# Attention values with their high and low parts side by side in one 128-column weight, and a new step order

## The reference

```
def one_block(qblk):                       # for each block of 128 queries
    sc = einsum('bqhgd,bkhd->bhgqk', qblk, k) * scale
    p = softmax(sc, axis=-1)
    return einsum('bhgqk,bkhd->bqhgd', p, v)

ya = blocked_attention(qa, ka, va, 1 / sqrt(64))
yb = blocked_attention(qb, kb, vb, 1 / sqrt(96))
merged = g_a * (ya @ w_branch_a) + g_b * (yb @ w_branch_b)
```

## Time and profile before

| what | value |
|---|---|
| median of 3 runs | 2993.85 us (2993.54 to 2993.94) |
| the profiled execution | 2993.22 us, its span 2991.4 us |
| PE busy | 2829.0 us, 95% of the span |
| DVE busy | 1614.9 us, 54% |
| ACT busy | 1147.8 us, 38% |
| POOL busy | 748.1 us, 25% |
| the chain that ended last | PE 86%, DVE 8%, ACT 2% |
| mean granted TensorE clock | 0.972 of full |

### The profile page before, as it was taken

One profiled execution on the slowest core, in us unless ns is written; L12 is line 12 of the kernel. 1 busy time (PEld: TensorE's weight loads), 2 busy tenths in 40 slices (PEclk: granted clock), 3 DMA queues, 4 the chain that ended last, 5 costly groups with the idle time before them and its releaser, 6 DMA issues.

```text
span 2991.4 us, 33731 instructions
## 1 busy us (share of the span) xinstructions
PE 2829.0 (95%) x12862; PEld 2317.4 (77%) x12862; DVE 1614.9 (54%) x2065; ACT 1147.8 (38%) x1758; POOL 748.1 (25%) x607
## 2 busy tenths in 40 slices
PE   8899999999998999999999967999999999999997
PEld 6677887888776778788887766878887789878886
DVE  5786446334367854453434895455533558555533
ACT  5675334222346753332223343322322348422221
POOL 2563113213025621140223161022200014122200
PEclk9999999999999999999999888999999989999999
DMA  3011322233220112223332201222232210123332
GB/s 136 28 43 43 99 92 85 94 97 99 85 85 22 43 53 95 85 92 99 99 95 87 79 19 60 92 92 95 96 106 99 83 52 1 57 92 99 99 103 88
DMA packets 75634, 236.68 MB, mean 79 GB/s; under 512 B 9776, under 2 KB 18240, under 8 KB 75488
## 3 DMA queue, kind: packets, MB, share of 16 engines
q1 hardware_dynamic: 74288, 231.31, 23.9%
q0 software_dynamic: 928, 3.27, 0.3%
q10 hardware_dynamic: 272, 0.06, 0.0%
HBM read 228.31 MB, written 2.10 MB: 77 GB/s over the span
## 4 chain that ended last, share of the span: by engine, by line
PE 86%; DVE 8%; ACT 2%; issue 1%; POOL 1%; DMA 1%; SPq 1%; DVEq 0%; POOLq 0%; ACTq 0%
PE bank L1800 27%; PE bank L1802 27%; PE bank L1801 27%; PE bank L2097 2%; PE bank L1961 1%; DVE S5S L1668 1%; DMA RAWW<-weights 1%; DVE STAT L1494 1%; PE bank L2003 1%; DVE S5S L1659 1%; SPq L817 1%; DVE WL L1383 1%; ACT WH L1072 1%; PE bank L1903 0%; DVE PHL L1388 0%
## 5 line engine op out<-in xcount | busy, mean ns | idle before, releaser
L1383 DVE TENSOR_TENSOR WL<-RAWW,WH 128x1024 fp32r<-128x1024 f32 (+2 forms) x424 | 573.7, 1357 | 862.5 <-ACT WH L1072 862.4
L1800 PE MATMUL bank<-UH,WH 128*128 128x512 f32 (+1 forms) x1920 | 762.3, 397 | 53.7 <-DVE UL L1393 29.4
L1801 PE MATMUL bank<-UL,WH 128*128 128x512 f32 (+1 forms) x1920 | 754.5, 393 | 0.0
L1802 PE MATMUL bank<-UH,WL 128*128 128x512 f32 (+1 forms) x1920 | 754.0, 393 | 0.0
L1072 ACT ACTIVATE WH<-RAWW 128x1024 fp32r<-128x1024 f32 (+2 forms) x424 | 433.9, 1027 | 368.5 <-DMA RAWW<-weights 368.0
L1800 PEld LDWEIGHTS bank<-UH,WH 128*128 128x128 f32 (+1 forms) x1920 | 364.6, 190 | 141.6 <-issue 58.1
L1801 PEld LDWEIGHTS bank<-UL,WH 128*128 128x128 f32 (+1 forms) x1920 | 365.0, 190 | 78.2 <-issue 2.4
L1802 PEld LDWEIGHTS bank<-UH,WL 128*128 128x128 f32 (+1 forms) x1920 | 364.4, 190 | 77.6
L1800 PE MATMUL bank<-HH,WH 128*128 128x512 f32 x512 | 199.2, 389 | 0.0
L1801 PE MATMUL bank<-HL,WH 128*128 128x512 f32 x512 | 199.2, 389 | 0.0
L1802 PE MATMUL bank<-HH,WL 128*128 128x512 f32 x512 | 199.2, 389 | 0.0
(11 more groups left out here) (340 smaller groups left out, 4711.2 us busy)
## 6 DMA issues: line engine op xcount, KB each, us to landing
RAWW<-weights SPq DMA_DIRECT2D x424, 512.0 KB, 3.4
X<-x SPq DMA_DIRECT2D x8, 256.0 KB, 5.4
FF<-tables POOLq DMA_DIRECT2D x2, 1024.0 KB, 7.2
U<-S5U SPq DMA_DIRECT2D x16, 128.0 KB, 2.4
GEL<-U SPq DMA_DIRECT2D x128, 16.0 KB, 1.8
out<-FF SPq DMA_DIRECT2D x8, 256.0 KB, 2.0
S5B<-s_b POOLq DMA_DIRECT2D x1, 512.0 KB, 4.3
S5C<-s_c POOLq DMA_DIRECT2D x1, 512.0 KB, 4.3
```

Source lines behind the costliest of these rows:

```text
L1383: dve.tensor_tensor(slot_words(WL, c % SLOTS, size), slot_words(RAWW, c % SLOTS, size), f32(slot_words(WH, c % SLOTS, size)), ALU.subtract ...
L1800: nc.tensor.matmul(out_, w[0], x_[0], start=start, stop=False, **how)
L1801: nc.tensor.matmul(out_, w[0], x_[1], start=False, stop=False, **how)
L1802: return nc.tensor.matmul(out_, w[1], x_[0], start=False, stop=stop, **how)
```

## The change

Of one head, the 64 columns of high value parts and the 64 columns of low parts now stand side by side in one weight of 128 columns (VS, MVS). Two products per key tile (`pair`: this weight with the high and with the low part of the probabilities) take the place of three, and OUTB then holds the result of the high values in 64 rows and that of the low values in the other 64. The two halves are added: ACT copies the low half across into a tile (`att_out_side`), DVE adds the other half from the bank (`att_out_sum`). After every second head ACT makes the high part of all 128 rows (`att_out_hi`) and POOL the low part (`att_out_lo`), where before ACT and DVE did this for each head. POOL's zeroing of MVH and MVL is gone. In the order, `att_lo` moves from behind the values to the start of a step, the exponential becomes a step of its own (`att_exp`) behind the transposes, and the transposes stand ahead of `att_normalise`. The gate phase's first products with QH, QL and with YBH, YBL get a wait for the low parts of their own.

```diff
# attention_steps: the order of the steps
-    for x in range(n + 8):
+    for x in range(n + 10):
         h, phase = divmod(x - KT - 4, KT)
         if 0 <= h < 2 * HEADS and phase == 3:
-            plan.add("att_out_hi", h=h, pv=h)
+            plan.add("att_out_side", h=h, pv=h)
+        if 2 <= h <= 2 * HEADS and h % 2 == 0 and phase == 1:
+            plan.add("att_out_lo", h=h - 1, p=whole.p)
...
+        if 4 <= x <= n + 3:
+            plan.add("att_lo", u=x - 4, h=(x - 4) // KT, t=(x - 4) % KT)
         if x < n:
             plan.add("att_scores", "u", h=x // KT, t=x % KT)
+        if 3 <= x <= n + 2:
+            plan.add("att_transpose", u=x - 3, h=(x - 3) // KT, t=(x - 3) % KT)
+        if x < n:
+            plan.add("att_exp", u=x)
         if 1 <= x <= n:
             plan.add("att_normalise", u=x - 1)
-        if 3 <= x <= n + 2:
-            plan.add("att_transpose", u=x - 3, h=(x - 3) // KT, t=(x - 3) % KT)
...
-        if 4 <= x <= n + 3:
-            plan.add("att_lo", u=x - 4, h=(x - 4) // KT, t=(x - 4) % KT)
         if 0 <= h < 2 * HEADS and phase == 3:
-            plan.add("att_out_lo", h=h, pv=h)
+            plan.add("att_out_sum", h=h, pv=h)
+        if 2 <= h <= 2 * HEADS and h % 2 == 0 and phase == 0:
+            whole = plan.add("att_out_hi", "p", h=h - 1, pv=h - 1)
# tiles
-        VH = at("VH", A0 + 20, [P, KT, P], F32R)
-        VL = at("VL", A0 + 22, [P, KT, P], F32R)
+        VS = at("VS", A0 + 20, [P, KT, 4, HD], F32R)
+        FIRST_SUM = at("FIRST_SUM", A0 + 32, [P, SEQ])
...
-        MVH = at("MVH", A0 + 60, [P, 2, KT, P], F32R)
-        MVL = at("MVL", A0 + 64, [P, 2, KT, P], F32R)
+        MVS = at("MVS", A0 + 60, [P, 2, KT, 2, HD], F32R)
...
+        def out_sum(st):
+
+            return SPARE[:, 0, :] if st.h >= 2 else FIRST_SUM[:]
# POOL
-                elif st.kind == "mla_mm" and st.h == 0:
-                    value_zeros(l)
...
+                elif st.kind == "att_out_lo":
+                    h, lo_, _, k = pv_place(st.h)
+                    pool.wait_ge(y_h.sem, y_h.after(l, st.p))
+                    pool.tensor_tensor(lo_[:, k, :], out_sum(st), f32(h[:, k, :]), ALU.subtract).then_inc(y_l.sem, 1)
# ACT
-                elif kind == "att_scores":
+                elif kind == "att_exp":
...
+                elif kind == "att_out_side":
+                    rows = pv_place(st.h)[2]
+                    other = slice(HD - rows.start, P - rows.start)
+                    act.wait_ge(pv.sem, pv.after(l, st.pv))
+                    if st.h >= 2:
+                        act.wait_ge(y_l.sem, y_l.after(l, st.h // 2 - 1))
+                    act.activation(out_sum(st)[rows, :], OUTB[other, :], ACT.Copy).then_inc(y_side.sem, 1)
                 elif kind == "att_out_hi":
                     h, _, rows, k = pv_place(st.h)
-                    act.wait_ge(pv.sem, pv.after(l, st.pv))
-                    act.activation(h[rows, k, :], OUTB[rows, :], ACT.Copy).then_inc(y_h.sem, 1)
+                    act.wait_ge(y_sum.sem, y_sum.after(l, st.pv))
+                    act.activation(h[:, k, :], out_sum(st), ACT.Copy).then_inc(y_h.sem, 1)
# DVE
-                elif kind == "att_out_lo":
-                    h, lo_, rows, k = pv_place(st.h)
-                    dve.wait_ge(y_h.sem, y_h.after(l, st.pv))
-                    rest(lo_[rows, k, :], OUTB[rows, :], h[rows, k, :]).then_inc(y_l.sem, 1)
+                elif kind == "att_out_sum":
+                    rows = pv_place(st.h)[2]
+                    dve.wait_ge(y_side.sem, y_side.after(l, st.pv))
+                    dve.tensor_tensor(out_sum(st)[rows, :], OUTB[rows, :], out_sum(st)[rows, :], ALU.add).then_inc(y_sum.sem, 1)
# PE
+            def pair(out_, w, x_, start, stop, **how):
+
+                nc.tensor.matmul(out_, w, x_[0], start=start, stop=False, **how)
+                return nc.tensor.matmul(out_, w, x_[1], start=False, stop=stop, **how)
...
-                            pe.wait_ge(y_l.sem, y_l.after(l, st.h - 1))
-                    if st.h == HEADS and st.keys[0] == 0:
-                        pe.wait_ge(mv_zero, l + 1)
+                            pe.wait_ge(y_sum.sem, y_sum.after(l, st.h - 1))
...
-                        v = (VH[:, k, :], VL[:, k, :]) if st.h < HEADS else (MVH[:, st.h % 2, k, :], MVL[:, st.h % 2, k, :])
-                        ins = product(OUTB[:], v, (ph[:, k, :], pl[:, k, :]), k == 0, k == KT - 1)
+                        i = st.h % 2
+                        v = VS[:, k, 2 * i:2 * i + 2, :] if st.h < HEADS else MVS[:, i, k, :, :]
+                        ins = pair(OUTB[:], v.rearrange("p a n -> p (a n)"), (ph[:, k, :], pl[:, k, :]), k == 0, k == KT - 1)
```

More of the change, by code:

```diff
@@ L683, in build @@
         mats_cut = ctx.enter_context(nc.semaphore("mats_cut"))
-        mv_zero, k_zero = (ctx.enter_context(nc.semaphore(k)) for k in ("mv_zero", "k_zero"))
+        k_zero = ctx.enter_context(nc.semaphore("k_zero"))
         x_done = signal("x_done", "x", DT)
@@ L706, in build @@
         probs_h, probs_l = signal("probs_h", "u"), signal("probs_l", "u", 2)
-        pv, y_h, y_l = signal("pv", "pv"), signal("y_h", "pv"), signal("y_l", "pv")
+        pv, y_side, y_sum = (signal(k, "pv") for k in ("pv", "y_side", "y_sum"))
+        y_h, y_l = signal("y_h", "p"), signal("y_l", "p")
         gate = signal("gate", "ge")
@@ L833, in layer_inputs @@
                 ins.then_inc(k_zero, 1)
-            def value_zeros(l):
-                pool.wait_ge(pv.sem, pv.after(l, U_HEADS - 1))
-                for k in range(2):
-                    for v in (MVH, MVL):
-                        ins = pool.memset(f32(v[:, k, :, HD - k * HD:P - k * HD]), 0.0)
-                ins.then_inc(mv_zero, 1)
             def add_squared(l, k, again):
@@ L1832, in linear_job @@
                     for k in range(kt):
-                        if st.first:
+                        if st.first or st.half == 0 and i == k == 0:
                             pe.wait_ge(*ready(k0 + k))
```

31 lines of the change are left out of this document (15 added, 16 removed).

## The result

The changed kernel takes 3013.39 us, median of 4 runs (3013.26 to 3014.44), against 2993.69 for the kernel before in the same runs: a ratio of 1.0065, 95% interval 1.0053 to 1.0078. It is slower by 20 us where 7 to 8 were forecast, and lies 0.4 us above the range.

What follows compares the result with a forecast made beforehand. In the seven MLA loops a DVE-ACT-POOL loop without PE work was taken to bind, nearly level with PE. Per layer -2.5 + 8.0 - 1.5 = +4.0 us, +8 for both: 2993.2 + 8 = 3001 us, range 2982 to 3013.

Steps and rivals of the forecast that it cites:

- Until the first MQL: Each layer's stretch before the first MQL: fewer products, POOL's new instruction and the order together -2.5 us, bounds -5.7 and 0.
- The prediction's own sign: Before the first MQL: this part is wrong if PE's wait at the long L1444 (3.93 us) shrinks instead of growing.
- The seven loops: First MQL to last, per layer: order +2.9 and POOL's low part +5.0, together +8.0 us, bounds +4.0 and +11.
- Its signs: In the trace after, MQL starts about 12.9 and 14.1 us apart in turn, against 12.36.
- The order's term: In the loops: a second PHL before the second reciprocal, 6 x 0.7 less 1.3 of vanished waiting, +2.9 us.
- POOL's term: In the loops: `att_out_lo` inside POOL's unbroken work in four of seven, 4 x 1.26, +5.0 us.
- the sum above has that at x = 17 alone: POOL holding up RL, WL and L1444, DVE's two-SBUF-input steps, was counted only at x = 17, before the loops.
- No removed product lies in them: The seven loops: none of the removed products was taken to lie there, so nothing gained once PE is ahead.
- After the last MQL: Last MQL to gates, per layer: products -2.8 us, new wait for the sum and high part +1.3, together -1.5.
- is hidden: At the gates: POOL's last low part, 1.26 us, covered by 48 products, 11 us, before QH is read.
- the term of -2.8 us for the removed products: After the last MQL: 12 of the 64 removed products, PE bound or nearly so, save 2.8 us.
- a rival about the loops: Clock rival: PE idles at each MQL, half-clock spells lengthen loops, 14 us more, 3013 to 3015 us; chance 0.08.

Runs made afterwards that it cites:

- two_products: Kernel before without the product of low values and high probabilities; 2985.23 us, ratio 0.9970.
- order_only: Kernel before with only the new order of the steps of a key tile; 3006.27 us, ratio 1.0037.
- low_on_dve: Changed kernel with the low part of a pair's sum made on DVE instead of POOL, at the same step; 3007.07 us, ratio 1.0043.
- low_later: Changed kernel with POOL's low part moved behind the first normalisation, last pair unmoved, two sum tiles in turn; 2999.32 us, ratio 1.0013.
- rl_psum: Changed kernel with RL of the MLA heads made from PSUM tile TURN instead of SBUF tile FF; 3003.48 us, ratio 1.0031.
- low_twice: Changed kernel with POOL making the low part twice for the MLA pairs, once into an unused tile; 3023.34 us, ratio 1.0090.
- fill_after: Changed kernel with the product of values and low probabilities issued twice, giving PE its former work; 3019.03 us, ratio 1.0078.
- old_order: Changed kernel with the steps of a key tile in their former order; 3008.73 us, ratio 1.0046.
- values_only: Changed kernel with the former order of steps and the low part on DVE; 3016.73 us, ratio 1.0068.

## Why the prediction was wrong in size

**Until the first MQL: the number came, the working didn't.** -2.5 forecast and measured in layer 0, -2.0 in layer 1. The kernels that change one part at a time put it together otherwise: two_products alone gives -1.4 for the 3.4 us counted for products, order_only gives -1.9 for 0.3, and moving the low part from POOL to DVE (low_on_dve, first MQL at 161.28) gives back none of the 1.26 charged for it. The prediction's own sign speaks against the step too: PE's wait of 3.93 us behind the long L1444 is gone. The same instruction, L1455 now, takes 0.80 us for 3.59, and PE has several shorter waits instead (1.35 at 123.94, 1.21 at 127.90, 2.11 at 131.81). That the sum came out is luck.

```profile
120.94 0.80 DVE L1455 SCALAR_TENSOR_TENSOR CF<-CF,LP,RCQ 128x512 f32<-128x512 f32 x1
```

**The seven loops: right in cause, mis-sized**, +8.0 for +10.2. Its signs came: MQL 13.2 to 13.5 us apart without a low part and 13.9 to 14.5 with one, for 12.9 and 14.1. The two terms share POOL's row and can't be told apart in one way only. By the place of the low part (changed kernel against low_later) it costs 6.4 us for 5.0, and the rest of the change 3.9 (90.4 for 86.5) for 2.9. By the order alone (order_only) the order costs 5.9, and what comes on top 4.3. Both ways miss the same thing. The order's term had one effect of the order, the second PHL, which the trace shows (0.7 us) and which costs some 0.25 us a loop at most, as far as the runs tell. It left out RL, which now meets POOL's unbroken row: in all seven loops of order_only, and in the three loops of the changed kernel without a low part, at 2.1 to 2.8 us. rl_psum takes 0.9 us off each of these three. In the four others ACT makes the pair's whole high part ahead of RH, RL comes later and takes 1.1 us. POOL's term had the low part's length, and the dose of low_twice confirms that (1.24 and 1.23). It left out that the row then runs into WL, 0.5 us in three loops. The prediction had the rule for both, with RL and WL named, and put it at nothing beside L1444: "the sum above has that at x = 17 alone". That is the step that failed. The Trainium skill, SBUF — State Buffer, Who interferes with whom, says a DVE instruction with two SBUF inputs contends with a GpSimd instruction that reads SBUF; 2.79 us with FF and 0.68 with TURN at the same place agree. The section gives no price for a DVE instruction that meets a row of them: here RL let a whole further POOL instruction go first (221.06 to 222.34), and was done only with the third under way.

One reading was wrong without changing the sum: "No removed product lies in them". Of the 64 products 24 and 12 were counted outside the loops, so 28 lie inside, and PE has 386 matmuls there for 420. Nothing waits for them, as fill_after shows.

**After the last MQL: -1.5 forecast, +0.5 measured.** The chain of side copy, sum and high part put UH 1.27 us later behind the last product, as reckoned. What was costed at nothing, POOL's last low part ("is hidden"), wasn't: it runs at 278.63, beside DVE's first UL, which has two SBUF inputs and takes 1.25 us for 0.75. The end of the attention in the changed kernel, PE, DVE and ACT by start, answering to the earlier trace rows:

```profile
276.14 0.40 PE L1817 MATMUL bank<-PHL,MVS 128*128 128x512 f32 x1
...
276.57 0.59 ACT L1193 ACTIVATE SPARE<-bank 64x512 f32<-64x512 f32 x1 [2.99 <-PE bank L1817]
277.92 0.63 ACT L1197 ACTIVATE YBH<-SPARE 128x512 fp32r<-128x512 f32 x1 [0.76 <-DVE SPARE L1517]
278.46 3.16 ACT L1093 ACTIVATE UH<-X,LP 128x512 fp32r<-128x512 f32 x5
...
279.19 1.91 DVE L1404 SCALAR_TENSOR_TENSOR UL<-X,LP,UH 128x512 fp32r<-128x512 f32 x2 [1.31 <-ACT UH L1093]
...
280.59 0.66 PE L1810 MATMUL bank<-UH,WH 128*128 128x512 f32 x1 [4.05 <-DVE UL L1404]
281.05 0.63 PE L1811 MATMUL bank<-UL,WH 128*128 128x512 f32 x1
...
284.31 0.40 PE L1810 MATMUL bank<-UH,WH 128*128 128x512 f32 x1
```

A wait of 4.05 us for a forecast of 3.6. The larger part of the miss here is the term of -2.8 us for the removed products, which was taken as on the path: the 2.8 us of products saved turned into waiting: PE has 1.7 us less work in this stretch and idles 2.3 us more (7.5 for 5.2 by the two tables of stretches).

**The clock behind the gates: no price given.** Matmuls are 0.43 us apart from 281.05 to 284.04, for 0.23 before. The first nine take 3.7 us for 2.15, 1.6 us more, of which 1.3 are left later on. The forecast had the longer wait, had the half clock behind the earlier trace rows and had its price (1.8 us for a spell), but put the clock only into a rival about the loops. That rival was wrong for this kernel: longer spells at half clock came in two of the seven loops (0.87 over loops 4 and 6), and fill_after, with a clock of 1.00 there, shows that these have the same length without them. In old_order and values_only such spells do set the length of loops.

**The rivals.** PE isn't the bound of the loops (two_products). The forecast time failed by the terms named: 2.2 us in the loops, 2.0 behind them and 1.3 at the gates, 5.5 in layer 0; in layer 1 6.2, with 0.5 less won ahead of the first MQL. Together 11.7 us, of the 11.8 by which the span missed the forecast.

## What to carry to other kernels

Before an instruction is put on POOL, or moved on DVE, list the DVE instructions with two SBUF inputs that then stand beside POOL's work. Price each by what is left of POOL's row and not by its own length: RL, 0.68 us long, lost 2.2 us here. The same POOL instruction cost 1.2 to 1.7 us in the row and nothing three steps on. Look for the idle time of the target engine inside the loop and aim for it, and past DVE's two-input steps. Where a wait ahead of a long row of matmuls grows from 2.3 to 4 us, reckon with half clock behind it: in these traces it came in 20 of 22 cases for 3 of 16, and left the changed kernel 1.3 us later in each layer.
